# RWKV output kept with tokens in the rows: two groups of small matmuls turned round, and the head norm done per 128-token tile on VectorE

## The reference

```python
y_t = jnp.einsum('dbhvk,dbhk->dbhv', S, r_t)        # output of each step, both directions d
...
y = y[0] + jnp.flip(y[1], axis=1)
mean = jnp.mean(y, axis=-1, keepdims=True)          # over the 64 channels of a head
var = jnp.mean(jnp.square(y - mean), axis=-1, keepdims=True)
y = ((y - mean) * lax.rsqrt(var + LNX_EPS)).reshape(B, T, D_RWKV)
y = y * lnx_w + lnx_b                               # per channel
y = y + (bonus[..., None] * v).reshape(B, T, D_RWKV)
return y * g
```

## Time and profile before

| | |
|---|---|
| median of 3 runs | 2459.87 us (2453.34 to 2466.22) |
| profiled execution, its own time | 2454.77 us |
| its span, first to last instruction | 2453.0 us |
| PE busy over the span | 2298.1 us (94%) |
| mean granted TensorE clock | 0.969 of full |

### The profile page before, as it was taken

How to read it: one execution, slowest core, us unless ns; L and a number is a source line. 1 busy time by engine, 2 the same in 40 slices (tenths; PEclk the granted TensorE clock), 3 DMA queues, 4 the chain that set the end, 5 groups by cost and what they waited for, 6 DMA issues and landing times. The chain is left out here.

```text
span 2453.0 us, 64850 instructions
## 1 busy us (share of the span) xinstructions
PE 2298.1 (94%) x28182; PEld 1520.8 (62%) x28182; DVE 1029.8 (42%) x2157; ACT 704.9 (29%) x1398; POOL 401.1 (16%) x504
## 2 busy tenths in 40 slices
PE   7989999899999999999968899997799999999997
PEld 4444444356556666556647756664688888888883
DVE  3236767633554644645647534444111111111115
ACT  4134545433544453534512112221000000000003
POOL 0012222200000000000011000002543433333331
PEclk9999999999999999999988899998899999999999
DMA  4113434533343343432358333242899999999996
GB/s 136 34 48 121 135 133 144 185 68 87 88 107 89 90 114 72 115 98 65 105 186 287 112 108 112 78 157 76 309 326 356 335 356 332 359 352 340 363 315 223
DMA packets 351772, 436.49 MB, mean 178 GB/s; under 512 B 164512, under 2 KB 283440, under 8 KB 343344
## 3 DMA queue, kind: packets, MB, share of 16 engines
q1 hardware_dynamic: 335168, 397.94, 47.6%
q0 software_dynamic: 14256, 35.04, 5.6%
q10 hardware_dynamic: 2112, 0.01, 0.1%
HBM read 329.87 MB, written 102.93 MB: 176 GB/s over the span
## 5 line engine op out<-in xcount | busy, mean ns | idle before, releaser
L1130 PE MATMUL m_ps_pp<-hT,r_wcol 128*128 128x512 f32 x864 | 428.4, 621 | 9.0 <-PEq L348 9.0
L489 PE MATMUL r_pp<-hT,r_wcol 128*128 128x512 f32 x720 | 314.2, 596 | 9.3 <-DMA r_wcol<-in_w_in_dram 8.0
L2602 PE MATMUL e_ps_gu<-e_xT,e_wg 128*128 128x128 f32 x2048 | 236.8, 277 | 18.3 <-DVE e_xT L2677 18.3
L489 PEld LDWEIGHTS r_pp<-hT,r_wcol 128*128 128x128 f32 x720 | 136.2, 191 | 177.6 <-issue 166.1
L2602 PEld LDWEIGHTS e_ps_gu<-e_xT,e_wg 128*128 128x128 f32 x2048 | 234.1, 194 | 18.8 <-DVE e_xT L2677 18.8
L2602 PEld LDWEIGHTS e_ps_gu<-e_xT,e_wu 128*128 128x128 f32 x2048 | 233.6, 192 | 14.8 <-issue 14.8
L1130 PEld LDWEIGHTS m_ps_pp<-hT,r_wcol 128*128 128x128 f32 x864 | 148.7, 191 | 140.0 <-issue 129.1
L2602 PE MATMUL e_ps_gu<-e_xT,e_wu 128*128 128x128 f32 x2048 | 233.8, 275 | 0.0
L2611 PE MATMUL e_ps_y<-e_wd,e_hid 128*128 128x512 f32 x512 | 225.1, 592 | 1.1 <-DVE e_hid L2691 1.1
L2055 PE MATMUL o_ps_out<-o_wout,y 128*128 128x512 f32 x384 | 178.6, 610 | 5.0 <-DVE y L2261 5.0
L2684 DVE TENSOR_SCALAR e_y<-e_ps_y,e_row 128x512 f32<-128x512 f32 x32 | 24.0, 751 | 337.8 <-PE e_ps_y L2611 305.0
(11 more groups left out here) (354 smaller groups left out, 3348.9 us busy)
## 6 DMA issues: line engine op xcount, KB each, us to landing
e_wg<-in_moe_w_gate_dram SPq DMA_DIRECT2D x32, 2048.0 KB
e_wu<-in_moe_w_up_dram SPq DMA_DIRECT2D x32, 2048.0 KB, 14.6
e_wd<-in_moe_w_down_dram SPq DMA_DIRECT2D x32, 2048.0 KB
r_wcol<-in_w_in_dram SPq DMA_DIRECT2D x35, 512.0 KB, 5.6
ar<-r_ar SPq DMA_DIRECT2D x24, 512.0 KB, 2.7
kb<-r_kb SPq DMA_DIRECT2D x24, 512.0 KB, 2.7
m_ar<-ar SPq DMA_DIRECT2D x48, 256.0 KB, 4.9
m_kb<-kb SPq DMA_DIRECT2D x48, 256.0 KB, 3.9
```

The costliest lines, as they stand in the source:

```text
L489: last = nc.tensor.matmul(pp[k % SPANS][:], wcol[q][:, c], self.hT[:, c, s * SPAN:(s + 1) * SPAN], start=c == 0, stop=c == KT - 1)
L1130: last = nc.tensor.matmul(pp[n % 2][:], wcol[(k + 2) % 3][:, c], self.hT[:, c, span(s)], start=c == 0, stop=c == KT - 1)
L2602: last = nc.tensor.matmul(ps[:, q * P:(q + 1) * P], w[u][:, c, q * P:(q + 1) * P], xT[u][:, c * P:(c + 1) * P], start=c == 0, stop=c == KT ...
```

## The change

The two output groups of the scan swap weights and streamed operand, so that `ps_o` holds 32 tokens of one direction in each quarter of the rows and 64 channels for each head in the columns. The order of the calls is that of the new list `by_turn`. ScalarE's copy has the same size; the store becomes four DMAs for four chunks, with pieces of 256 channels, into `ytok` (tokens in the rows). In the second stage an item is a tile of 128 tokens by 512 channels. The two matmuls with ones and the spreading copy go; DVE sums over 64 columns for mean and squares, and multiplies by the inverse root in two halves (`even`, `odd`), which also put the heads in their place. TensorE then transposes the normed values, ACT applies scale and shift out of PSUM with four instructions, and DVE adds the bonus and multiplies by the gate in a step of its own, `r_gate`, one filler round later. The costs written in the list are unchanged. Loads of bonus and gate are cut by tile.

```diff
-            oacc = [sb(f"m_oacc{u}", [P, G, P]) for u in range(2)]
+            oacc = [sb(f"m_oacc{u}", [P, 4, 2, 2 * RH]) for u in range(2)]
...
-            ps_o = ps_x[:, :, M * RH:M * RH + M * CH].rearrange("p w (m t) -> p w m t", t=CH)
-            ps_ru = ps_x[:, :, M * RH + M * CH:].rearrange("p w (i v) -> p w i v", v=RH)
+            ps_o = ps_x[:, :, M * RH:M * RH + 2 * RH].rearrange("p w (i v) -> p w i v", v=RH)
+            ps_ru = ps_x[:, :, M * RH + 2 * RH:].rearrange("p w (i v) -> p w i v", v=RH)
...
     def store_o(c):
         self.waits(sp, act_c.at("O", c))
         for d in range(2):
-            sp.dma_start(self.yT[d, 0:PAIRS, :, (c - 3) * CH:(c + 1) * CH].rearrange("j p t -> p j t"),
-                         oacc[c // 4 % 2][:, d * PAIRS:(d + 1) * PAIRS]).then_inc(out_stored, 16)
+            chunks = slice(c - 3, c + 1), slice(step_of(c), step_of(c - 3) + 1)
+            by_pos = self.ytok[d].rearrange("(c t) (pos n) -> t pos c n", t=CH, pos=2)[:, :, chunks[d]]
+            for pos in range(2):
+                sp.dma_start(by_pos[:, pos, WAY[d]], oacc[c // 4 % 2][quad[2 * pos + d]].rearrange(
+                    "t c w n -> t c (w n)")).then_inc(out_stored, 16)
...
+    by_turn = [(i, d, w, c) for i in range(2) for d in range(2) for w in range(2) for c in range(2)]
...
-        for d, i, w, h in units:
-            g, m = 4 * d + 2 * i + w, 2 * d + i
-            last = nc.tensor.matmul(ps_o[heads[h], w, m], state[c % 2][heads[h], g],
-                                    ar[c % RING][heads[h], g, CH:2 * CH], start=m == 0, stop=False,
+        for i, d, w, h in by_turn:
+            g = 4 * d + 2 * i + w
+            last = nc.tensor.matmul(ps_o[quad[2 * (h ^ w) + d], w, i], ar[c % RING][heads[h], g, CH:2 * CH],
+                                    state[c % 2][heads[h], g], start=i == 0, stop=False,
                                     skip_group_check=True)
...
-        for d, i, w, k in units:
-            r, g, m = heads[k], 4 * d + 2 * i + w, 2 * d + i
-            last = nc.tensor.matmul(ps_o[heads[k ^ w], w, m], vz[c % 2][r, g], sm[c % RING][r, g, CH:],
+        for i, d, w, k in by_turn:
+            r, g = heads[k], 4 * d + 2 * i + w
+            last = nc.tensor.matmul(ps_o[quad[2 * k + d], w, i], sm[c % RING][r, g, CH:], vz[c % 2][r, g],
                                     start=False, stop=True, skip_group_check=True)
...
-            self.waits(eng, dve_c.at("grown", c), (out_stored, 16 * 2 * (c // 4 - 1)) if c >= 8 else None)
-            nc.scalar.activation(by_way(oacc[c // 4 % 2])[:, :, :, c % 4 * CH:(c % 4 + 1) * CH], ps_o,
-                                 ACT.Copy).then_inc(*act_c.inc("O"))
+            self.waits(eng, dve_c.at("grown", c), (out_stored, 16 * 4 * (c // 4 - 1)) if c >= 8 else None)
+            nc.scalar.activation(oacc[c // 4 % 2][:, c % 4], ps_x[:, :, M * RH:M * RH + 2 * RH], ACT.Copy
+                                 ).then_inc(*act_c.inc("O"))
...
-for i in range(ITEMS + 3):
-    for name, k, cost in (("r_sum", i + 1, 0), ("r_mean", i, 1.0), ("n_sq", i, 0), ("n_ss", i - 1, 0.9),
-                          ("n_inv", i - 1, 0), ("n_wide", i - 2, 1.1)):
+for i in range(ITEMS + 4):
+    for name, k, cost in (("r_sum", i + 1, 0), ("n_inv", i - 2, 0), ("r_mean", i, 1.0), ("n_sq", i, 0),
+                          ("n_ss", i - 1, 0.9), ("n_wide", i - 2, 1.1), ("r_gate", i - 3, 0)):
...
     def load_y(k):
         if k >= ITEMS:
             return
-        s, i, u = k // PAIRS, k % PAIRS, k % RING_B
+        u, rows = k % RING_B, self.ytok[:, tile(FINISHED[k])]
         self.waits(sp, pool_sum.ago("sum", k, RING_B))
-        sp.dma_start(y[:, i, span(s)], self.yT[0, i, :, span(s)]).then_inc(y_loaded[u], 16)
-        sp.dma_start(ob[u][:], self.yT[1, i, :, span(slot(1, s))]).then_inc(y_loaded[u], 16)
+        sp.dma_start(rwkv(k), by_k(rows[0])).then_inc(y_loaded[u], 16)
+        sp.dma_start(ob[u][:], rows[1]).then_inc(y_loaded[u], 16)
 
     def load_g(k):
         if k >= UNITS:
             return
         u = k % RING_G
         if is_r(k):
-            s, i = k // PAIRS, k % PAIRS
             self.waits(sp, dve_r.ago("gated", k, RING_G))
-            sp.dma_start(bv[u][:], self.bonusv[i, :, span(s)]).then_inc(g_loaded[u], 16)
-            sp.dma_start(gt[u][:], self.rgate[i, :, span(s)]).then_inc(g_loaded[u], 16)
+            for dst, src_of in ((bv, self.bonusv), (gt, self.rgate)):
+                sp.dma_start(by_k(dst[u][:]), src_of[:, :, tile(FINISHED[k])].rearrange("j p t -> p j t")
+                             ).then_inc(g_loaded[u], 16)
...
-    def r_mean(k):
-        self.waits(eng, pool_sum.at("sum", k), bank_x.free(("mean", k)))
-        nc.tensor.matmul(ps_x[:], self.headsum[:], y[:, k % PAIRS, span(k // PAIRS)], start=True, stop=True
-                         ).then_inc(bank_x.made, 1)
-
     def n_ss(k):
-        self.waits(eng, act_sq.at("sq", k), bank_y.free(("ss", k)))
-        w = 2 if is_r(k) else 1
-        ones = self.headsum[:, 0:P:RH] if is_r(k) else self.allsum[:, 0:1]
-        for i in range(PAIRS):
-            last = nc.tensor.matmul(ps_y[:, w * i:w * i + w], sq[k % 2][:, i * P:(i + 1) * P], ones,
-                                    start=True, stop=True)
-        last.then_inc(bank_y.made, 1)
+        if not is_r(k):
+            self.waits(eng, act_sq.at("sq", k), bank_y.free(("ss", k)))
+            for i in range(PAIRS):
+                last = nc.tensor.matmul(ps_y[:, i:i + 1], sq[k % 2][:, i * P:(i + 1) * P], self.allsum[:, 0:1],
+                                        start=True, stop=True)
+            last.then_inc(bank_y.made, 1)
...
-        self.waits(eng, act_wide.at("wide", k), bank_x.free(("wide", k)))
+        self.waits(eng, dve_norm.at("odd", k) if is_r(k) else act_wide.at("wide", k - ITEMS),
+                   bank_x.free(("wide", k)))
...
-                self.waits(eng, (wout_loaded, 16 * KY), dve_r.at("gated", ITEMS - 1))
-            self.waits(eng, dve_h.at("gated", n), dve_x.ago("x1", n, 1))
+                self.waits(eng, (wout_loaded, 16 * KY))
+            self.waits(eng, dve_r.at("gated", n), dve_h.at("gated", n), dve_x.ago("x1", n, 1))
...
     def n_inv(k):
-        heads = 2 * PAIRS if is_r(k) else PAIRS
-        self.waits(eng, dve_inv.at("inv", k), bank_x.full(("wide", k - 2)))
-        nc.scalar.activation(wide[k % 2][:].rearrange("p (h n) -> p h n", h=heads),
-                             var[k % 2][:, 0:heads].unsqueeze(2).broadcast_to((P, heads, SPAN // heads)),
-                             ACT.Copy).then_inc(*act_wide.inc("wide"))
+        if not is_r(k):
+            self.waits(eng, dve_inv.at("inv", k), bank_x.full(("wide", k - 2)))
+            nc.scalar.activation(by_k(wide[k % 2][:]), var[k % 2][:, 0:PAIRS].unsqueeze(2).broadcast_to(
+                (P, PAIRS, P)), ACT.Copy).then_inc(*act_wide.inc("wide"))
+
+    def n_wide(k):
+        if is_r(k):
+            self.waits(eng, bank_x.full(("wide", k)), (scales_loaded, 16 * 3))
+            for i in range(PAIRS):
+                last = nc.scalar.activation(rwkv(k)[:, i], ps_x[:, i * P:(i + 1) * P], ACT.Identity,
+                                            scale=lnw[:, i:i + 1], bias=lnb[:, i:i + 1])
+            last.then_inc(bank_x.read, 1)
...
     def r_mean(k):
-        rows = y[:, k % PAIRS, span(k // PAIRS)]
-        self.waits(eng, bank_x.full(("mean", k)))
-        nc.vector.scalar_tensor_tensor(rows, ps_x[:], -1.0 / RH, rows, ALU.mult, ALU.add
-                                       ).then_inc(bank_x.read, 1)
+        self.waits(eng, pool_sum.at("sum", k))
+        nc.vector.tensor_reduce(mean[k % 2][:].rearrange("p (b i) -> p b i", i=2), by_head(rwkv(k)), AX_X,
+                                ALU.add).then_inc(*dve_mean.inc("mean"))
+        self.waits(eng, dve_mean.at("mean", k))
+        nc.vector.scalar_tensor_tensor(by_head(rwkv(k)), each_head(mean[k % 2][:]), -1.0 / RH, by_head(rwkv(k)),
+                                       ALU.mult, ALU.add).then_inc(*dve_mean.inc("centred"))
 
     def n_ss(k):
-        heads, size, eps = (2 * PAIRS, RH, EPS_R) if is_r(k) else (PAIRS, P, EPS_H)
-        self.waits(eng, bank_y.full(("ss", k)), act_wide.ago("wide", k, 2))
-        nc.vector.tensor_scalar(var[k % 2][:, 0:heads], ps_y[:, 0:heads], 1.0 / size, eps, ALU.mult, ALU.add
-                                ).then_inc(bank_y.read, 1)
+        r = var[k % 2]
+        if is_r(k):
+            self.waits(eng, act_sq.at("sq", k))
+            nc.vector.tensor_reduce(r[:], sq[k % 2][:].rearrange("p (h n) -> p h n", n=RH), AX_X, ALU.add
+                                    ).then_inc(*dve_var.inc("sumsq"))
+            self.waits(eng, dve_var.at("sumsq", k))
+            nc.vector.tensor_scalar(r[:], r[:], 1.0 / RH, EPS_R, ALU.mult, ALU.add
+                                    ).then_inc(*dve_var.inc("var"))
+        else:
+            self.waits(eng, bank_y.full(("ss", k)), act_wide.ago("wide", k - ITEMS, 2))
```

(51 more changed lines are left out.)

27 lines of the change are left out of this document (14 added, 13 removed).

## The result

The changed kernel takes 2465.57 us (median of 7 runs, 2464.66 to 2469.81) beside 2455.67 of the kernel before (7 runs, 2452.03 to 2466.22). The ratio is 1.0031, 95% interval 1.0016 to 1.0046: about 8 us slower by the ratio (the two medians are 9.9 apart), where 8 us faster was forecast. A second measurement gave 1.0042 (1.0025 to 1.0059).

The account below looks back on a forecast made before the run. PE alone was taken to bound the scan; PE, DVE and DMA together the norm items. Scan -17, last store +0.5 and norm +8.5 give -8 us on the 2459.9 median: 2452, range 2433 to 2474.

Parts of the forecast that it names:

- forecast -0.52: Scan, output group in `solve` with the scores: 1.39 to 1.5 us instead of 1.96, a gain of 0.52 per chunk.
- forecast +0.17: Scan, turned output group in `grow`: a cost of 0.17 us per chunk from wider streaming and a shape change.
- rival (c): Scan, turned group in `grow` runs two places at a time: +0.64 us per chunk, total 2475 us; chance 0.13.
- PE work alone sets this stage, and a microsecond saved on PE there is a microsecond: RWKV scan: PE busy 713.0 of 722 us, so savings count in full, -17 us over 48 chunks.
- the length of a step as DVE's busy time plus 4 x 1.4 us and some tenths for sums and loads: Norm stretch: DVE's 20.7 us per scan step becomes 26.3; steps of 31 instead of 27.1 us, +8 for two.
- the gain at the start: Start of the norm stretch: PE no longer sits 4.2 us behind POOL's third sum, -4 us.
- DVE over 85% busy: Norm stretch, sign of being right: DVE busy over 85% between 1240 and 1350 in the profile after.
- PE waiting at the transposes for the second half multiply: Norm stretch, a sign of being right in the profile after; no size given.
- ACT's four copies as hidden: Norm: ACT loses one 512-column copy and gains four of 128; busy 15.5 of 54 us, which hides that.
- (d): Norm items: DVE and loads choke them, +24 us, total +7.5, 2467 us; chance 0.12.
- (b): Norm items: PE held them too, so without its 29.5 us items give -6, total -23, 2437 us; chance 0.30.
- (e): Scan gain replaced by another wait, 2469 us, or partly lost as row halves sharing a bank exclude each other, 2464; chance 0.07.

Follow-up runs that it names:

- after_again: The changed kernel measured once more, unaltered; ratio to the kernel before 1.0042.
- all three edits: Changed kernel with transposes first and a round late, bonus and gate loads at r_gate's place, and a round over two gaps; ratio to before 0.9898, repeated 0.9924.
- warm: Changed kernel with twelve 128x128 identity matmuls added on PE ahead of each wait of the transposes; ratio to before 1.0065.
- wide_late: Changed kernel with the transposes one round later and the halves where they were; ratio to before 0.9985.
- the loads freed by themselves: Changed kernel with bonus and gate loads issued at r_gate's place on SP's queue instead of n_wide's; ratio to before 1.0053.
- mean_cost: Changed kernel with r_mean's planning cost 2.0 instead of 1.0, so one round takes two gaps; ratio to before 1.008.
- the free loads: Changed kernel with transposes first and a round late, plus bonus and gate loads at r_gate's place, old planning costs; ratio to before 0.9995.
- the two gaps: Changed kernel with transposes first and a round late, plus n_ss planned at 2.0 so a round takes two gaps; ratio to before 0.9987.
- the first edit: Changed kernel with the transposes first in a round and a round late, nothing else; ratio to before 1.000.
- scan_alone: Kernel before with only the scan's part of the change, the norm as before (output wrong); ratio to before 0.9945.

## Why the prediction was wrong

**The scan's groups: right.** One chunk of the changed kernel without a pause, PE's timeline:

```profile
600.63 0.45 PE L1193 MATMUL m_ps_x<-m_state,m_ar 64*32 64x64 f32 x32
...
615.48 0.45 PE L1193 MATMUL m_ps_x<-m_state,m_ar 64*32 64x64 f32 x32
615.86 1.10 PE L1154 MATMUL m_ps_s<-m_ar,m_kb 64*64 64x128 f32 x32
616.89 1.12 PE L1134 MATMUL m_ps_pp<-hT,r_wcol 128*128 128x512 f32 x2
617.95 0.69 PE L1202 MATMUL m_ps_x<-m_v,m_kbt 64*64 64x64 f32 x32
618.58 0.67 PE L1206 MATMUL m_ps_x<-m_v,m_sm 64*32 64x64 f32 x32
619.18 0.65 PE L1164 MATMUL m_ps_b<-m_px,m_pw 32*32 32x64 f32 x32
```

and the same chunk before:

```profile
601.62 1.06 PE L1190 MATMUL m_ps_x<-m_ar,m_state 64*64 64x32 f32 x30
...
616.83 1.06 PE L1190 MATMUL m_ps_x<-m_ar,m_state 64*64 64x32 f32 x30
```

From L1193's start to the projection's is 1.41 us, against 1.96: -0.55, forecast -0.52. From L1202 to L1164 is 1.23, against 1.07: +0.16, forecast +0.17. L1206 has 0.67 from first start to last end, forecast 0.68, so rival (c) fell, and from L1193 to the next group it is 0.38, forecast 0.39, although both row halves write one bank. The Trainium skill ("TensorEngine Tiling (Array Packing)", Restrictions and Gotchas) says that they can't at the same time; the measurement decides. The chunk went from 15.21 to 14.85, -0.36 for a forecast of -0.35. (The reduction of the earlier trace rows, by which the sum over 64 columns was priced, lies between 1400 and 1735, not after 1735; each of the two sums then took 0.68 us, forecast 0.70.)

**The scan as a whole: mis-sized.** 47 such chunks would give 16.9 us; the traces show 8.3. The step that failed is "PE work alone sets this stage, and a microsecond saved on PE there is a microsecond". The waits of PE between 521 and 1228, after:

```profile
PE m_ps_x L1202 <- issue: 4.7, 4, 1.4
PE m_ps_b L1164 <- issue: 1.9, 4, 0.9
PE m_ps_x L1190 <- issue: 1.8, 2, 1.1
PE m_ps_x L1193 <- issue: 1.7, 3, 0.7
PE m_ps_x L1177 <- issue: 1.3, 1, 1.3
PE m_ps_x L1206 <- issue: 1.3, 2, 0.8
PE m_ps_s L1154 <- issue: 1.2, 3, 0.4
```

13.9 us of pauses in which nothing visible held PE, where the five such groups before add up to 7.2. That takes 6.7 of the 16.9; 1.9 stays unaccounted for. PE's busy time from the group's first to its last start fell by 14.8 us, from 710.4 to 695.6, for a forecast of 16; in `after_again` it was 699.6. The prediction called the 2.1 us of the earlier trace rows the sum of PE's longest waits; it is the largest of five groups, which add up to 7.2. I had read them as too small to matter, and took no care that they might grow. The scan of the turned kind took 706.1 to 717.4 us in sixteen profiles (mean 711.3), that of before 718.8, 719.1 and 719.2.

**The norm: the step that decided.** What failed is the length of a step as DVE's busy time plus 4 x 1.4 us and some tenths for sums and loads. It gave two steps of 31 us and one of 20.5, +8.5 with the gain at the start. Measured were 31.9, 38.8 and 27.2 us, +26.6 with the start and the fourth step. The prediction had DVE's work itself right: 5.0 us per item by the operations' own rows (0.68 and 0.68 for the two sums, 0.69 for the centring, 0.84 for the halves, 0.75 and 0.95 for bonus and gate, 0.42 for the small ones), 4.9 forecast. But it took the parts of an item to overlap as they did before, put the wait of PE for the halves at nothing, and forecast DVE over 85% busy; DVE was 79% and 66% busy in the two longest steps, and the wait was 45.6 us. The timeline of the changed kernel at one item shows what the sum left out:

```profile
1315.36 1.09 PE L2015 MATMUL o_ps_k<-ident,e_wd 128*128 128x128 f32 x4
1315.58 1.23 DVE L2204 TENSOR_TENSOR e_wd<-o_ps_s,g_mask 128x1024 f32<-128x1024 f32 x1 [6.33 <-PE o_ps_s L2008]
...
1316.72 0.68 DVE L2266 TENSOR_TENSOR y<-y,o_bv 128x512 f32<-128x512 f32 x1
1317.44 0.69 DVE L2268 TENSOR_TENSOR y<-y,o_gt 128x512 f32<-128x512 f32 x1
1318.05 0.20 DVE L2254 RECIPROCAL o_var<-o_var 128x8 f32<-128x8 f32 x1
...
1318.28 0.76 DVE L2261 TENSOR_TENSOR o_wide<-y,o_var 128x256 f32<-128x256 f32 x2
...
1319.09 0.48 PE L2048 MATMUL o_ps_x<-ident,o_wide 128*128 128x128 f32 x1 [2.64 <-DVE o_wide L2261]
```

DVE waited 6.33 us for PE's scores. Then PE stood while DVE did the mask, the bonus and gate of an older item, and only then the halves. With `n_inv` and `n_wide` of one item in one gap, and the small work of PE that lay between (mean and sum of squares) gone, PE and DVE take turns at every item, twelve waits for twelve items. The kernel with all three edits does the same work on every engine in another order and is about 30 us faster, so the order is the cause and not the amount of DVE's work. That the 29.5 us of small PE work had been cover for DVE is my reading and not shown: no run put it back, and in `warm` other PE work filled much of the wait and gained nothing. The prediction did name PE waiting at the transposes for the second half multiply as a sign of being right, but gave it no term in its sum. It also took ACT's four copies as hidden; in `wide_late` PE waited 27.0 us behind them.

**The rivals.** The result is that of (d) in its number (2467, measured 2465.6), and that is luck: (d) has the full 17 us of the scan and +24 for the norm, and the traces show 8.3, +26.6 and 7.4 back in later steps. Its cause, loads and DVE at their limits, is not what the runs showed either: the loads freed by themselves gave no gain, and DVE's share of the four long steps was lower than before (69% against 78%). (b), PE as the holder of the items, fell: PE had 29.5 us less to do and the steps grew. (e) was half right for the scan, by a mechanism that it did not name. The 4 us at the start came as 2.2 and 0.4.

**Settled and open.** Shown: the norm's part costs some 21 us, in this order of work and not by the amount of it; behind PE's wait for the halves stand others (ACT's copies in `wide_late`, a late load in `mean_cost`); and only all three edits together bring the kernel clearly under the one before. Open: why the late steps got a better clock in the changed kernel (twice, 23.7 us for the last one in both profiles, 29 before), 1.9 us of the scan, what the low clock costs by itself, whether DVE or the DMAs bound the best order, and what makes an instruction fetch late.

## What to carry to other kernels

When work moves from one engine to another, don't only add it up there: ask what the old place was covering, write down for each gap which engine reads what another wrote in it, and count the gap by the planned costs, not by the row of the list. A lockstep hides the next one: here the free loads and the two gaps added nothing to the first edit one by one and 0.8 to 1.0% together; follow each wait that takes the place of the one removed, and try them combined before giving up. A reader should be at least one gap behind its writer: in the same gap the wait for the halves was 29.5 to 45.6 us here, one gap apart 1.1, 3.1, 20.7 and 24.8, two apart 1.8 to 4.1. A load's wait must not stand on a queue in front of loads that have nothing to do with it.

## What the hardware showed beside that

PE's unexplained pauses come at fixed places. In the changed kernel's scan there are nineteen pauses over 0.15 us without a releaser, and from one to the next the matmuls number a multiple of 127 within four (1270, 3175, 3937, 258, 631, 380, ...); so it is with the eleven before. (In `scan_alone` one of thirteen lies elsewhere.) The row of the instruction queue for this stretch is:

```profile
q8 instruction: 148, 2.42, 1.4%
```

Those are packets and MB: 148 of 16 KB for some 18,800 matmuls and as many weight loads: 254 instructions each, that is 127 matmuls. Such packets land 3.3 to 8.1 us apart, and eighteen of the nineteen pauses ended 1.2 to 1.55 us after one had landed (the other 5.8 us after), as here, where one landed at 1118.03:

```profile
1117.80 0.46 PE L1202 MATMUL m_ps_x<-m_v,m_kbt 64*64 64x64 f32 x14
1119.44 0.50 PE L1202 MATMUL m_ps_x<-m_v,m_kbt 64*64 64x64 f32 x18 [1.19 <-issue]
```

As I read it, PE had run out of instructions. The Trainium skill ("Runtime: NRT & Kernel Launch", Instruction fetch mechanics) has blocks of 256 instructions, 16 KiB each, which agrees to within two, and says that the fetch is hidden behind the rate of issue, which this trace contradicts by 14 us. That faster groups make more of these pauses fits the change from 7 to 14 us, but the experiment that was to break up the short groups left them, so what decides it is not settled.
